# Second mixer of a two-layer decoder trunk: the convolution and its gate matmuls by pairs of channel chunks, and zero matmuls ahead of the first projection

## The reference, cut to what matters

```python
proj = (h @ w_in)
c_q, c_k, c_v, c_g, d_x, d_gate = split_cols(proj, ODD_SPLITS)
q, k = rope(c_q), rope(c_k) * C_DK ** -0.5
...                                   # retention over q, k, c_v; gated by silu(c_g)
xp = jnp.pad(d_x, ((0, 0), (D_CONV - 1, 0), (0, 0)))
xc = conv_b
for j in range(D_CONV):               # 4 taps, causal
    xc = xc + xp[:, j:j + L, :] * conv_w[j]
r = sigmoid(einsum(xc by blocks of 64, w_r) + b_r)
i = sigmoid(einsum(xc by blocks of 64, w_i) + b_i)
a = exp(-RGLRU_C * r * softplus(-lam))
u = sqrt(1 - a * a) * (i * xc)        # then a scan over the tokens, gated by gelu(d_gate)
```

## Time and profile before

| | before |
|---|---|
| median of 3 runs | 1164.35 us (1162.38 to 1164.51) |
| profiled execution, its own time | 1159.1 us |
| its span | 1157.3 us |
| TensorE busy | 870.3 us, 75% |
| VectorE busy | 354.0 us, 31% |
| ScalarE busy | 262.2 us, 23% |
| main transfer queue, share of the 16 DMA engines | 91.8% |
| moved | 443.05 MB, 383 GB/s on the mean |
| mean granted TensorE clock | 0.945 of full |

### The profile page before, as it was taken

One profiled execution on the slowest core, in us unless ns is written; L12 is line 12 of the kernel. 1 busy time (PEld: TensorE's weight loads), 2 busy tenths in 40 slices (PEclk: granted clock), 3 DMA queues, 4 the chain that ended last, 5 costly groups with the idle time before them and its releaser, 6 DMA issues.

```text
span 1157.3 us, 25416 instructions
## 1 busy us (share of the span) xinstructions
PE 870.3 (75%) x10392; PEld 549.2 (47%) x10393; DVE 354.0 (31%) x838; ACT 262.2 (23%) x500; POOL 6.8 (1%) x16
## 2 busy tenths in 40 slices
PE   9999987776766666666678998877666666666665
PEld 8988964433333333333358896444333333333332
DVE  6899741211111111111137774121111111111112
ACT  6656531110001000000035744111000000000002
POOL 0000000000000000000000000000000000000000
PEclk9999999999889898989899999999988989998999
DMA  9744689999999999999998298999999999999996
GB/s 339 268 163 167 244 341 420 426 428 425 428 430 428 428 429 429 428 427 430 427 403 309 92 415 349 422 426 426 425 430 428 429 430 428 428 429 429 427 428 255
DMA packets 46579, 443.05 MB, mean 383 GB/s; under 512 B 4032, under 2 KB 5504, under 8 KB 20800
## 3 DMA queue, kind: packets, MB, share of 16 engines
q1 hardware_dynamic: 46256, 441.53, 91.8%
q10 hardware_dynamic: 144, 0.52, 0.1%
q0 software_dynamic: 128, 0.26, 0.1%
HBM read 441.25 MB, written 1.05 MB: 382 GB/s over the span
## 4 chain that ended last, share of the span: by engine, by line
DMA 54%; PE 33%; DVE 5%; ACT 4%; issue 3%; SPq 1%; DVEq 0%; ACTq 0%
DMA up_pairs<-in_moe_w_dram 47%; PE low_banks L1183 11%; DMA weights<-in_moe_w_dram 7%; PE sums_of_x L750 3%; PE low_banks L1199 3%; PE sums_of_x L752 3%; PE sums_of_x L751 3%; PE low_banks L1157 2%; PE low_banks L750 1%; PE low_banks L751 1%; PE low_banks L752 1%; DVE w_lo L1634 1%; PE low_banks L952 1%; PE sums_of_x L1210 1%; PE sums_of_x L1213 1%
## 5 line engine op out<-in xcount | busy, mean ns | idle before, releaser
L1183 PE MATMUL low_banks<-up_pairs,gates 128*32 128x256 f32 x4096 | 283.3, 438 | 128.4 <-DMA up_pairs<-in_moe_w_dram 118.8
L1183 PEld LDWEIGHTS low_banks<-up_pairs,gates 128*32 128x32 f32 x4096 | 143.3, 125 | 252.8 <-DMA up_pairs<-in_moe_w_dram 129.7
L1199 PE MATMUL low_banks<-weights,gates 128*32 128x256 f32 x2048 | 124.2, 382 | 85.4 <-DVE gates L2052 42.8
L2050 DVE TENSOR_TENSOR gates<-gates,low_banks 128x128 f32<-128x128 f32 x64 | 18.4, 287 | 411.1 <-ACT gates L1245 411.1
L1199 PEld LDWEIGHTS low_banks<-weights,gates 128*32 128x32 f32 x2048 | 64.3, 109 | 145.4 <-issue 81.2
L1245 ACT ACTIVATE gates<-low_banks 128x128 f32<-128x128 f32 x64 | 17.7, 277 | 427.7 <-PE low_banks L1183 427.7
L2045 DVE TENSOR_TENSOR gates<-low_banks,vecs 128x256 f32<-128x256 f32 x64 | 27.2, 424 | 257.6 <-PE low_banks L1166 257.6
L1157 PE MATMUL low_banks<-tok,gates 128*32 128x256 f32 x1024 | 68.5, 385 | 12.5 <-issue 8.8
L1634 DVE TENSOR_TENSOR w_lo<-weights,w_hi 128x2048 fp32r<-128x2048 f32 x28 | 64.0, 2287 | 20.3 <-ACT w_hi L1306 20.1
L1470 ACT COPY gates<-low_banks 128x256 f32<-128x256 f32 x64 | 23.8, 372 | 191.4 <-PE low_banks L1199 191.4
L1464 ACT COPY gates<-low_banks 128x256 f32<-128x256 f32 x64 | 23.8, 372 | 158.0 <-PE low_banks L1157 158.0
(11 more groups left out here) (298 smaller groups left out, 1132.9 us busy)
## 6 DMA issues: line engine op xcount, KB each, us to landing
up_pairs<-in_moe_w_dram SPq DMA_DIRECT2D x122, 2048.0 KB, 33.9
weights<-in_moe_w_dram SPq DMA_DIRECT2D x62, 2048.0 KB, 40.1
up_pairs<-in_moe_w_dram SPq DMA_DIRECT2D x12, 1024.0 KB, 31.8
weights<-in_even_w_in_dram SPq DMA_DIRECT2D x5, 2048.0 KB, 11.2
weights<-in_odd_w_in_dram SPq DMA_DIRECT2D x4, 2048.0 KB, 20.6
weights<-in_moe_w_dram SPq DMA_DIRECT2D x4, 1024.0 KB, 39.0
weights<-in_even_w_in_dram SPq DMA_DIRECT2D x3, 1024.0 KB, 10.8
weights<-in_even_w_out_dram SPq DMA_DIRECT2D x1, 2048.0 KB, 8.1
```

What stands on the lines that cost most here:

```text
L1183: ins = pe.matmul(bank[2][PASS * j:PASS * (j + 1), 0:T], got_T[:, k % 2, k // 2, :], up[:, k, :, j * P:(j + 1) * P], start=(k == 0), stop= ...
L1199: ins = pe.matmul(bank[3][PASS * q:PASS * (q + 1), T:2 * T], hid_T[:, c, :], down[:, c, q * T:(q + 1) * T], start=(c == 0), stop=(c == Q - 1),
```

## The change

- Six calls' worth of zero matmuls (12 instructions) into bank 0 stand ahead of `first_channels(1)`.
- VectorE scales and convolves chunks 0 and 1, then chunks 2 and 3. Within a pair a tap waits for the tap before it on the same chunk with one other operation between them, instead of three. The square of `scale` goes behind the convolution.
- TensorE does both gates for pair 0, then the rope swap, then both gates for pair 1. The wait for ScalarE's four sigmoids ahead of step 5 becomes a wait for six within step 5, ahead of the third channel chunk, where bank 0 is written again.
- ScalarE applies the sigmoids pair by pair, and the tanh waits for six of them.

```diff
             def odd_mixer():
+                keep_warm(6, 0)
                 first_channels(1)
...
+                def open_gates(pair):
+                    pe.wait_ge(conv_done, 2 * pair + 2)
+                    for g in range(2):
+                        for j in range(2):
+                            m = 2 * pair + j
+                            ins = pe.matmul(bank[2 * g + pair][:, j * T:(j + 1) * T], w_rg[:, g, m, :],
+                                            xc[:, m * T:(m + 1) * T], start=True, stop=True)
+                        ins.then_inc(rg_ready, 1)
+
+                def gates_read(m):
+                    if m == 2:
+                        pe.wait_ge(rg_gated, 6)
+
                 pe.wait_ge(rg_loaded, 64)
-                pe.wait_ge(conv_done, 4)
-                for g in range(2):
-                    for m in range(4):
-                        ins = pe.matmul(bank[2 * g + m // 2][:, m % 2 * T:m % 2 * T + T], w_rg[:, g, m, :],
-                                        xc[:, m * T:(m + 1) * T], start=True, stop=True)
-                    ins.then_inc(rg_ready, 1)
-
+                open_gates(0)
                 pe.wait_ge(qk_kept, 4)
                 pe.wait_ge(consts_loaded, 32)
                 for j in range(2):
                     pe.matmul(bank[4 + j][:, :], const("swap"), raw[:, j * 512:(j + 1) * 512],
                               start=True, stop=True).then_inc(swapped, 1)
-                pe.wait_ge(rg_gated, 4)
-                for i in (5, 6):
-                    by_channel(1, i, (6, 7, 0, 1))
+                open_gates(1)
+                by_channel(1, 5, (6, 7, 0, 1), gates_read)
+                by_channel(1, 6, (6, 7, 0, 1))
...
                 link(dve.tensor_copy(row, bank[1][:, 0:T]))
                 dve.wait_ge(dx_kept, 4)
-                link(tt(dx[:, :, 3:3 + T], dx[:, :, 3:3 + T], row.unsqueeze(1).to_broadcast([P, 4, T]), ALU.mult))
+                for pair in range(2):
+                    both = slice(2 * pair, 2 * pair + 2)
+                    link(tt(dx[:, both, 3:3 + T], dx[:, both, 3:3 + T], row.unsqueeze(1).to_broadcast([P, 2, T]), ALU.mult))
+                    for j in range(CONV):
+                        for n in range(2):
+                            m = 2 * pair + n
...
+                                dve.wait_ge(vector_step, steps[0] - (1 if j < CONV - 1 else 1 - n))
+                                ins = stt(o, dx[:, m, j:j + T], w, o, ALU.mult, ALU.add)
...
                 tt(scale_2[:, :], scale[:, :], scale[:, :], ALU.mult).then_inc(scale_2_set, 1)
...
-                for g, (dst, name) in enumerate(((rr, "b_r"), (ii, "b_i"))):
-                    act.wait_ge(rg_ready, g + 1)
...
-                act.wait_ge(rg_gated, 4)
+                for pair in range(2):
+                    for g, (dst, name) in enumerate(((rr, "b_r"), (ii, "b_i"))):
+                        act.wait_ge(rg_ready, 2 * pair + g + 1)
+                        for j in range(2):
+                            m = 2 * pair + j
+                            f(dst[:, m * T:(m + 1) * T], bank[2 * g + pair][:, j * T:(j + 1) * T], ACT.Sigmoid,
+                              bias=vec(name, m, m + 1)).then_inc(rg_gated, 1)
+
+                act.wait_ge(rg_gated, 6)
```

More of the change, by code:

```diff
@@ L1411, in odd_mixer @@
                 round_step(1, 6)
-                for g, (dst, name) in enumerate(((rr, "b_r"), (ii, "b_i"))):
-                    act.wait_ge(rg_ready, g + 1)
-                    for m in range(4):
-                        f(dst[:, m * T:(m + 1) * T], bank[2 * g + m // 2][:, m % 2 * T:m % 2 * T + T], ACT.Sigmoid,
-                          bias=vec(name, m, m + 1)).then_inc(rg_gated, 1)
-                act.wait_ge(rg_gated, 4)
+                for pair in range(2):
[6 more added lines that the diff above has]
+                act.wait_ge(rg_gated, 6)
                 for m in range(4):
@@ L1886, in odd_mixer @@
                 dve.wait_ge(dx_kept, 4)
-                link(tt(dx[:, :, 3:3 + T], dx[:, :, 3:3 + T], row.unsqueeze(1).to_broadcast([P, 4, T]), ALU.mult))
-                tt(scale_2[:, :], scale[:, :], scale[:, :], ALU.mult).then_inc(scale_2_set, 1)
[L1890 to L1902, removed]
+                for pair in range(2):
[4 more added lines that the diff above has]
+                            m = 2 * pair + n
+                            o = xc[:, m * T:(m + 1) * T]
+                            w = vec("conv_w", 4 * j + m, 4 * j + m + 1)
+                            if j == 0:
+                                mark(ts(o, dx[:, m, 0:T], w, vec("conv_b", m, m + 1), ALU.mult, ALU.add))
+                            else:
+                                dve.wait_ge(vector_step, steps[0] - (1 if j < CONV - 1 else 1 - n))
+                                ins = stt(o, dx[:, m, j:j + T], w, o, ALU.mult, ALU.add)
+                                if j < CONV - 1:
+                                    mark(ins)
+                                else:
+                                    ins.then_inc(conv_done, 1)
+                tt(scale_2[:, :], scale[:, :], scale[:, :], ALU.mult).then_inc(scale_2_set, 1)
                 rest_step(1, 5)
```

## The result

The changed kernel's median is 1153.37 us (1152.67 to 1154.89, 5 runs), and that of the kernel before 1162.38 us (5 runs, the three shown ahead and two more). By the ratio of the runs made side by side it takes 0.994 of the time (95% interval 0.9922 to 0.9958): faster by 7.0 us, 4.9 to 9.1. The profiled execution took 1153.37 us, span 1151.5, against 1157.3. The direction was as forecast. The time was not: 1159.2 was forecast, and the lower end of the range was 1156.5.

A forecast was written before the change was run, and what follows sets the result against it. TensorE's chain was taken to bound the mixer, its saving reaching the end through the transfer stream. Pairs 4.3 us plus zeros 0.8 made 5.1, off the 1164.35 median: 1159.2 us; 8-in-10 range 1156.5 to 1162.8.

The forecast's parts named there:

- the sum for the pairs: Second mixer, convolution and gates by pairs: step 5 starts 4.3 us earlier, from shorter idleness and gates at full clock.
- The zeros free of cost: Ahead of the first projection: 12 zero matmuls take about 1.5 us inside a 1.93 us TensorE wait, costing nothing.
- the zeros give nothing: First projection: clock mostly stays up without zeros, or falls with them too; 4.3 us saved, time 1160.0; chance 0.17.
- a stalled VectorE: Convolution taps: closer dependence makes step 5's low part 1.4 us later; gain 2.9 to 3.7, about 1161 us; chance 0.18.
- a hidden saving: Transfer stream at the end goes on as it is, so the mixer's saving does not show; time 1164; chance 0.10.
- "slower": VectorE's convolution: each of 12 taps costs over 0.62 us more, giving 1167 us and up; chance 0.05.
- the sum had 5.1: Total saving in the mixer: 4.3 us from the convolution by pairs plus 0.8 from the zeros.
- The second spell's price: Gates after the convolution wait: 2.97 us at half clock become full, 1.45 us saved.
- the first spell: Half clock at the first projection, 603.47 to 606.85 us: removal worth 1.6 us, counted at half, 0.8.
- The rival "More": First spell in most executions and gone entirely, second costlier elsewhere: 6 to 7.5 us saved, 1157 to 1158; chance 0.07.
- The wait's own share: TensorE's waits at gates and step 5: 3.80 us of idleness become 0.9, 2.9 saved.
- The wait of 0.27 us ahead of pair 1's gates: TensorE after the swap: idle 0.27 us until the convolution of pair 1 is done at 631.18 us.

## Why the prediction was wrong

**What held.** That TensorE's chain is the mixer and that all of it reaches the end: 5.7 us in the stretch, 5.8 in the span, transfers 5.6 earlier. In that pair of profiles the sum for the pairs is right too: step 5 began 10.5 us after step 4's end and begins 6.1 after it, 4.35 less where 4.3 was worked out. The zeros free of cost: 1.48 us in the wait, with 0.51 left. Pair 0 ready at 3.75 us (3.76), gates 0.18 us after step 4 (0.15), 1.80 us for its gates (1.75), step 5 at 632.11 - 626.00 = 6.1 us after step 4 (6.1). The rival that the zeros give nothing has eight profiles against it, in which the clock stayed up behind them. The rivals of a stalled VectorE and of a hidden saving are refuted, by the taps at 0.397 us and by the earlier transfers; the "slower" one with the first of them.

**What failed** is the price of the clock and the time that the saving was taken off; the mechanism was right. The saving was 7.0 us where the sum had 5.1. The interval of 4.9 to 9.1 just holds 5.1, so the size of the saving alone would not have put the time outside the range; the base did the rest.

- *The second spell's price.* This is the step of the sum that failed: the term "2.97 us at half clock become full (1.45 saved)" was read from one execution and taken as what the wait always costs. It is 1.4 to 3.0 us, 2.2 on the mean of four. With the first spell (1.5 in two profiles of four, 0.75 on the mean, where the sum had 0.8) the clock costs the stretch 2.95 us where the sum had 2.25. So the stretch gives 49.67 - 43.89 = 5.8 us and not 5.1. The rival "More" named this cause, with 0.07.
- *The wait's own share* came out right, 2.83 against 2.9, but by parts that offset each other. The wait of 0.27 us ahead of pair 1's gates never came and that of 0.48 ahead of step 5 was 0.28, while gates and swap took 0.4 longer than in one block. Step 5 starts when VectorE has its low part ready, and the time of that was forecast rightly; what TensorE does until then is waiting or work.
- *A spell that the sum did not have.* In routing the kernel before lost 1.65 us to a spell in three profiles of four, the changed kernel in none of three: 1.2 us of the difference between the means. The first profile happened to have none, so no row asked for it. Over the other kernels it is no rule: it is in two of those seven (the zeros alone; twice the zeros), so part or all of the 1.2 may be chance.
- *The base.* I took the saving off a median of three runs, 1164.35. With two more it is 1162.38, and in three later sets of 17 to 24 runs 1160.7 to 1161.4. Of the 5.8 us by which 1159.2 is too high, 2 to 3.6 are there and 1.9 in the saving; with the 2, what is left is the distance between the medians' 9.0 and the ratio's 7.0. That the profiled execution lay 5.25 us below the median was the warning: its mean granted clock was 0.945, against 0.939, 0.942 and 0.938 in the three others profiled later. The prediction noted the distance and went on.
- *The chance of the first spell* was taken from eight gaps of 1.49 to 2.05 us. The clock fell behind the three shortest, of 1.49, 1.57 and 1.66 us, and held behind the five others; the three next to the mixer's 1.93 us (1.90, 1.93 and 1.94) all held. So nothing there gave the half that was counted, and that it came out near that in the mixer (two of four profiles of the kernel before) is luck. Two of the three at which it fell, and the shortest at which it held:

```profile
312.89 5.35 PE L1183 MATMUL low_banks<-up_pairs,gates 128*32 128x256 f32 x64 [1.66 <-DMA up_pairs<-in_moe_w_dram]
356.94 5.35 PE L1183 MATMUL low_banks<-up_pairs,gates 128*32 128x256 f32 x64 [1.49 <-DMA up_pairs<-in_moe_w_dram]
832.84 3.66 PE L1183 MATMUL low_banks<-up_pairs,gates 128*32 128x256 f32 x64 [1.72 <-DMA up_pairs<-in_moe_w_dram]
```

The chances given add up to 1.01, which changes nothing.

The mean span of four profiles of the kernel before (1157.3, 1160.4, 1160.2, 1162.1) is 1160.0, that of three of the changed one (1151.5, 1152.4, 1155.1) 1153.0. These 7.0 us divide into 5.8 in the mixer stretch and 1.2 in routing; ahead of the mixer 0.95 us more were gained and in the second layer's experts 0.94 lost, stretches that the change doesn't touch. That agrees with the timed 7.0, whose interval would allow 4.9 as well. The 5.8 is the part that experiments show; the 1.2 in routing is not shown to be the change's.

The Trainium skill, "TensorE: Matmul & The Clock Gate", section "Why this matters for your kernels", asks only that longer idle gaps than these be kept out. Read as a rule that a gap of 1.9 us leaves the clock up, it does not hold here: of six profiles without zeros the clock fell behind that gap in three, and in a fourth it had fallen just ahead of it. In the Trainium skill, "VectorE: DVE Perf Modes", section "The DRAIN you can't avoid", a semaphore between chained operations costs nothing extra. The pairs' taps agree: 0.397 us from start to start with a wait for the operation before last, 0.396 with looser waits. A wait for the operation just before does cost here: behind the scaling of pair 0 the next operation starts 0.04 us after its end (622.20 + 0.69, 622.93), while the taps start 0.08 us before the end of the one ahead.

**What stays open:** whether the changed kernel has fewer spells in routing for a reason, whether the additional wait in the last expert is why the clock falls at the first projection (it parts six profiles, and no run changes it by itself), why the medians lie 2 us further apart than the ratio says, and why the time ahead of and behind the mixer moves by 0.5 to 1 us between executions.

## What to carry to other kernels

Where an engine with a clock that drops stands behind a wait, price the wait and what follows it apart, and the second as a range: what followed the same wait of 3.8 us cost 1.4 us in one execution and 3.0 in another. One profile of a program whose runs spread over 5 us is one draw; if it lies at an edge of the runs, expect the terms to lie there too. Splitting a producer so that its consumer starts on half of it took both the wait and its aftermath away; filling both waits with zeros took only the aftermath, about half of the gain (3.8 of 7.1 us), for two lines.

## What the runs showed of the hardware

- TensorE's clock fell to 1.2 GHz behind a wait of 1.9 us in three profiles of six and just ahead of it in a fourth; these four had a further wait of 0.8 to 1.5 us some 3 us ahead of it, which the other two had not. With a wait of 3.8 us it fell, during it or up to 1.2 us behind it, in all six profiles that had it unfilled (the kernel before four times, the zeros alone, the wait put back). There it stayed at half for 3.4 us in four of them and for 6.8 in two.
- The length of the gap alone does not say whether the clock falls: in one profile it fell behind gaps of 1.49, 1.57 and 1.66 us and held behind five of 1.72 to 2.05 us.
- Where bf16 matmuls on zeros filled the wait, the clock stayed up: in all eight profiles with them at the first projection (of six without, four were at half there, one of them already before the wait), and in both with them ahead of the gates.
- A zero matmul of 256 columns in bf16 starts every 0.106 us, a product of the projection of the same width every 0.12.
